# The final norm's two products: from GpSimd and ScalarE to one VectorE operation per tile, in a two-layer streaming encoder on Trainium2

## The reference, cut to what matters

```python
def rmsnorm(x, g):
    xf = x.astype(jnp.float32)
    y = xf * lax.rsqrt(jnp.mean(xf * xf, axis=-1, keepdims=True) + NORM_EPS)
    return (y * g.astype(jnp.float32)).astype(x.dtype)

for l in range(DEPTH):
    ...
    h_p = h_p + hier_moe(rmsnorm(h_p, norm_ffn[l]).reshape(b * t, d), *mw).reshape(b, t, d)
    h_s = h_s + hier_moe(rmsnorm(h_s, norm_ffn[l]).reshape(bd * td, d), *mw).reshape(bd, td, d)
y_prompt = rmsnorm(h_p, norm_final)
y_sample = rmsnorm(h_s, norm_final)
```

## Time and profile before

| what | us |
|---|---|
| median of three runs (lowest, highest) | 1415.55 (1410.67, 1418.3) |
| the profiled execution | 1415.48 |
| its span, first to last instruction | 1413.7 |
| PE busy in the span | 1225.1 (87%) |
| DVE busy | 468.2 (33%) |
| ACT busy | 285.8 (20%) |
| POOL busy | 165.9 (12%) |

### The profile page before, as it was taken

The page is one execution under the profiler, slowest core; times in us unless marked ns, Lnnn a source line. Parts: engine busy times, 40 slices in busy tenths (PEclk is TensorE's granted clock), DMA queues, the critical chain, the costliest instruction groups (busy, mean ns, idle before and its releaser), DMA issues.

```text
span 1413.7 us, 30382 instructions
## 1 busy us (share of the span) xinstructions
PE 1225.1 (87%) x13325; PEld 774.2 (55%) x13325; DVE 468.2 (33%) x1125; ACT 285.8 (20%) x714; POOL 165.9 (12%) x216
## 2 busy tenths in 40 slices
PE   6988899958999999948998799989886999999960
PEld 4444355547777777724444444444546777777740
DVE  4477652251000000025356651374633000000007
ACT  2123252110000000012345530242310000000013
POOL 1211120010000000020122221110001000000014
PEclk9889899969999999969999799999876999999995
DMA  9100040069999999953003101030028999999943
GB/s 302 14 10 2 1 182 30 16 230 357 371 401 397 393 389 406 349 195 112 16 15 122 69 16 45 30 124 16 30 78 286 353 401 403 396 392 396 381 157 145
DMA packets 73427, 283.73 MB, mean 201 GB/s; under 512 B 20205, under 2 KB 21277, under 8 KB 65098
## 3 DMA queue, kind: packets, MB, share of 16 engines
q1 hardware_dynamic: 56190, 237.94, 43.8%
q0 software_dynamic: 9216, 31.11, 6.4%
q10 hardware_dynamic: 7884, 12.65, 2.6%
HBM read 257.20 MB, written 24.48 MB: 199 GB/s over the span
## 4 chain that ended last, share of the span: by engine, by line
PE 67%; DVE 10%; DMA 9%; issue 9%; POOL 3%; ACT 1%; SPq 0%; ACTq 0%; POOLq 0%; DVEq 0%
PE bank L1135 22%; PE bank L850 13%; PE bank L1151 10%; PE bank L1061 8%; DMA slot<-in_moe_w 6%; PE bank L1007 2%; PE bank L974 2%; PE bank L1120 2%; PE bank L881 2%; POOL slot L2089 2%; PE bank L983 1%; DVE h L1948 1%; DVE slot L1649 1%; DVE stats L1648 1%; PE bank L873 1%
## 5 line engine op out<-in xcount | busy, mean ns | idle before, releaser
L1135 PE MATMUL bank<-arena,slot 128*64 128x96 f32 x8192 | 355.6, 249 | 13.9 <-issue 7.4
L1135 PEld LDWEIGHTS bank<-arena,slot 128*64 128x64 f32 x8192 | 346.8, 139 | 21.8 <-issue 12.3
L850 PE MATMUL bank<-slot,xT 128*128 128x512 f32 x512 | 240.6, 626 | 4.5 <-ACT slot L1325 3.3
L850 PEld LDWEIGHTS bank<-slot,xT 128*128 128x128 f32 x512 | 100.5, 202 | 125.0 <-issue 123.0
L1932 DVE TENSOR_TENSOR arena<-arena,bank 128x384 f32<-128x384 f32 x32 | 17.7, 554 | 406.6 <-ACT arena L1430 207.7
L1151 PE MATMUL bank<-slot,arena 128*32 128x512 f32 x1056 | 137.1, 594 | 0.4 <-issue 0.4
L1061 PE MATMUL bank<-slot,normed 128*128 128x512 f32 x256 | 116.6, 609 | 2.6 <-issue 1.3
L1430 ACT ACTIVATE arena<-bank 128x384 f32<-128x384 f32 x32 | 15.7, 490 | 396.3 <-PE bank L1135 396.3
L1061 PEld LDWEIGHTS bank<-slot,normed 128*128 128x128 f32 x256 | 48.6, 195 | 59.0 <-issue 58.3
L2135 POOL DMA_INDIRECT arena<-normed_rows,arena x32 | 29.1, 908 | 408.1 <-PE bank L1120 374.0
L1151 PEld LDWEIGHTS bank<-slot,arena 128*32 128x32 f32 x1056 | 38.5, 110 | 66.9 <-issue 64.0
(11 more groups left out here) (181 smaller groups left out, 1148.8 us busy)
## 6 DMA issues: line engine op xcount, KB each, us to landing
slot<-in_moe_w SPq DMA_DIRECT2D x86, 2048.0 KB, 17.8
xT<-in_moe_w SPq DMA_DIRECT2D x10, 2048.0 KB, 23.8
slot<-in_w_in_odd SPq DMA_DIRECT2D x6, 2048.0 KB, 13.6
slot<-in_w_in_even SPq DMA_DIRECT2D x3, 2048.0 KB, 13.6
expert_rows<-arena ACTq DMA_DIRECT2D x32, 192.0 KB, 10.2
slot<-in_w_out_even SPq DMA_DIRECT2D x2, 2048.0 KB, 11.6
normed_rows<-slot POOLq DMA_DIRECT2D x8, 512.0 KB, 2.9
expert_rows<-arena ACTq DMA_DIRECT2D x32, 128.0 KB, 8.5
```

The lines of the kernel that those rows point to most:

```text
L850: last = nc.tensor.matmul(b[o:o + wide, 0:n], xT[:, k, P * t + o:P * t + o + wide], w[:, k, 0:n], start=(k == 0), stop=(k == KC - 1))
L1135: last = nc.tensor.matmul(bank[o:o + 64, b, CAP * m:CAP * m + CAP], weights(w[par])[:, k, at_:at_ + 64], xgT[:, par, k, :], start=(k == 0) ...
```

## The change

Step Z moves from ACT to DVE, and POOL's `gain` is gone. DVE's new step Z is one scalar_tensor_tensor per tile, `h` times the row's inverse root times `gfin`, five in all. `gained` is gone; the wait for `gfin_in` now stands on DVE.

```diff
--- before.py
+++ after.py
@@ -538,7 +538,6 @@
         rows_known = sem("rows_known")
         lists_in = sem("lists_in")
         mask_ready = sem("mask_ready")
-        gained = sem("gained")
         scale_ready = sem("scale_ready")
         fin_ready = sem("fin_ready")
         act_step = sem("act_step")
@@ -1477,13 +1476,6 @@
                     taken(act, key)
                     act.dma_start(dst[0, 0], row[0:HIST, :]).then_inc(out_pool, 16)
 
-            def step_Z(t):
-
-                act.wait_ge(gained, t + 1)
-                act.wait_ge(scale_ready, t + 1)
-                y = fin[0:ROWS[t], t, :]
-                nc.scalar.activation(y, y, ACT.Copy, scale=rstd[0:ROWS[t], 4, t:t + 1]).then_inc(fin_ready, 1)
-
             def step_lambda():
                 act.wait_ge(lam_dots, 1)
                 nc.scalar.activation(lam_exp, lam_dot, ACT.Exp).then_inc(lam_exps, 1)
@@ -1516,8 +1508,6 @@
                 elif kind == "experts":
                     experts(*a)
                     log_and_exp_table()
-                elif kind == "Z":
-                    step_Z(*a)
                 elif kind == "lambda":
                     step_lambda()
 
@@ -1950,6 +1940,14 @@
                       .then_inc(h_added, 1)
                     dve.wait_ge(h_added, 2 * NT * l + 2 * t + c + 1)
 
+            def step_Z(t):
+                r = ROWS[t]
+                if t == 0:
+                    dve.wait_ge(gfin_in, 16)
+                nc.vector.scalar_tensor_tensor(out=fin[0:r, t, :], in0=h[0:r, t, :], scalar=rstd[0:r, 4, t:t + 1],
+                                               in1=gfin[0:r, :], op0=ALU.mult, op1=ALU.mult)\
+                  .then_inc(fin_ready, 1)
+
             def experts(l):
                 full = crowded(dve, l)
                 with dve.If(full):
@@ -1989,6 +1987,8 @@
                     step_y(*a)
                 elif kind == "C":
                     step_C(*a)
+                elif kind == "Z":
+                    step_Z(*a)
                 elif kind == "R":
                     if a == [0, 0]:
                         dve.wait_ge(small_in, 16 * SMALL_LOADS)
@@ -2119,14 +2119,6 @@
                         link(ins)
                     src, width = dst, 2 * width
 
-            def gain(t):
-
-                r = ROWS[t]
-                if t == 0:
-                    pool.wait_ge(gfin_in, 16)
-                pool.wait_ge(h_added, 2 * NT + 2 * (t + 1))
-                gtt(fin[0:r, t, :], h[0:r, t, :], gfin[0:r, :], ALU.mult).then_inc(gained, 1)
-
             def own_tokens(l):
                 all_x_stored(pool, l)
                 for e in range(NE):
@@ -2167,8 +2159,6 @@
                     step_X(*a)
                 elif kind == "Us":
                     sums(*a)
-                elif kind == "C" and a[0] == 1:
-                    gain(a[1])
                 elif kind == "experts":
                     experts(*a)
 
```

## The result

The changed kernel takes 1404.45 us (median of eight runs, 1401.89 to 1407.05); the kernel before took 1415.67 us in the same series (eight runs, 1408.38 to 1418.84). The medians lie 11.2 us apart. The ratio, taken from the means, is 0.9926 with a 95% interval of 0.9906 to 0.9946: 0.74% faster, about 10.4 us. The least gain that the interval allows is 0.54%, so the gain is clear of the prediction's bound of 0.5%, but by little. The prediction said 1406.7, a gain of 8.8 us.

The account below looks back on a forecast made before the run. The prediction took the final norm's DVE chain, held by POOL's products, and POOL's late DRAIN as the bound. Gains of 5.6 us on the chain and 3.2 at POOL's end took 1415.48 to 1406.7 us; range 1402.5 to 1412.

Parts of the forecast that it names:

- the prediction's bound of 0.5%: Whole kernel: about 0.5%, here 7.1 us, is what a measurement can tell from no change.
- The hold: Final norm's Newton steps: POOL's product holds DVE's two-input operation, 5.21 us in X0 and 2.21 in X1; goes with the products.
- Rival (c): Final norm: the long DVE operation is not POOL's doing and stays; DVE carries 1.32 more per tile, 1417.4 us; chance 0.06.
- Z at 1.28 to 1.32: DVE's five new steps in the final norm: 1.32 us each from start to start, 1.28 for the last.
- The gather holding X0 for 0.32 us: Final norm's first Newton step: POOL's last gather instruction holds DVE until 1384.39, so its operation ends at 1384.42, not 1384.10.
- Gathers and ACT hidden: Final norm: gathers land before DVE's C steps need them, C3's with 2.6 us to spare; ACT's root has 0.4 to spare.
- POOL's end off the path: Program's end: POOL's DRAIN over by 1392.5 or 1396.0, no longer behind SP's; 3.2 us gained.
- The estimate of 8.1 us: Program's end, kernel before: POOL's DRAIN goes on for 8.1 us after POOL's last product, over at about 1405.4.
- Rival (a): Program's end: POOL's DRAIN waits for something there, so 3.3 us behind SP's drain stay; 1409.9 us; chance 0.21.
- (b): Program's end: DVE's two-input operations slow POOL's DRAIN, whose 8.1 us count from 1402.5; 1412.6 us; chance 0.09.
- The sum: Whole change: 8.8 us off the span, 5.6 on the chain and 3.2 from POOL's end; time 1406.7 us.
- Work from DVE to ACT: Final norm: skill's rule for a saturated DVE, set aside because 1.99 of its 5.25 busy us per tile is holding.

Follow-up runs that it names:

- the early and the late small product: Changed kernel plus one 32x1 POOL product: early, behind Z1, one run, 1407.58 us; late, at the very end behind Z4, 1411.59 us.

## Why the prediction was right, point by point

- **The hold was POOL's, through DVE's second input, and went with the products.** Right: shown by putting them back (both holds return), by memsets (no hold) and by one-input operations (the hold moves). Rival (c), the hold staying, is out: L1545 is short in all 25 places.
- **Z at 1.28 to 1.32.** The length was right, 1.283. The distance was not: I took 1.32 from start to start from two operations with a semaphore between them. Behind Z, DVE does not wait for Z's own end, and the next operation starts 1.20 behind its start (1382.67 to 1383.87), below even the lower bound of 1.28. Four times 0.12 is 0.5 us.
- **The gather holding X0 for 0.32 us.** Wrong, and it was an inference from one row. The earlier trace rows show L1555 starting half a microsecond ahead of the product and not getting through, from which I took it that the gather held it. Without products it passes beside the gather in 0.22, in five profiles. In the kernel with the products kept, too, L1546 began 0.53 ahead of the first product's record and was held. So the hold seems to begin before the record of POOL's product: by at least 0.3 us, since an operation of 0.22 would have been through by then (1384.41 against 1384.72). How much more is not shown. With this term and the one above (0.32 + 0.48 = 0.80) the predicted 18.79 us from X0 to the end of Z4 becomes 17.99; measured 18.04. What is left is small slips: the sum for X0 leaves out the 0.03 us between the end of L1555 and L1557, X takes 0.83 per tile where 0.81 was counted, and C4 takes 2.61 where 2.64 was. The Trainium skill's inference (SBUF — State Buffer, "Who interferes with whom"), that descriptor generation does not take the read side, stands by these five profiles.
- **Gathers and ACT hidden.** Right: DVE has no gap from 1381.84 to 1399.88.
- **POOL's end off the path, worth 3.2 us.** Right: from the end of the last scaling to the end of the span it was 5.6 us before and is 2.3 now. The estimate of 8.1 us rested on POOL's last product before, which ends at 1405.43:

```profile
1403.09 2.34 POOL L2128 TENSOR_TENSOR normed<-h,slot 32x1024 f32<-32x1024 f32 x1 [3.10 <-DVE h L1948]
```

  The DRAIN itself was 7.992, four times, in kernels where it begins with nothing ahead of it, and its end lay 8.1 to 8.2 us behind that of POOL's last operation. Rival (a), that POOL's end keeps its distance, is out by the early and the late small product. So is (b): beside a DVE that never pauses, the DRAIN of the early product still took 7.992.
- **The sum.** Predicted tail 21.2, measured 20.4; predicted gain 8.8 us, 9.6 by the trace, 10.4 by the runs with an interval from 7.6 to 13.3. Both mis-sized terms erred the same way, so nothing cancelled. Of the 2.25 us by which the median came out below 1406.7, 0.8 are theirs; the rest lies within the scatter of the runs and speaks neither for nor against the prediction.
- **Work from DVE to ACT.** The prediction set this aside because 1.99 of DVE's 5.25 us was holding. That left out what comes after the change: without the holds DVE still runs 18 us without a gap, and the Newton step on ACT took 2.2 us off the tail.

## What to carry to other kernels

A cheap operation that is long in one place is not dear but blocked: look what another engine was doing until the same moment, and ask which of its neighbours pass. Work moved off DVE onto GpSimd can cost more than it saves while DVE's own operations need two inputs from SBUF; here 1.2 us per tile on DVE replaced a product of 2.3 that stopped it, and work that DVE does itself can be cheaper than work that it is kept waiting for. And the end of a program is a race between engines: the last store is not the end if another engine's own finish comes later, and in a program like this one GpSimd should have its last work more than 8 us before the last store has landed.

## What the runs showed of the hardware that I had not expected

- POOL's DRAIN at the program's end takes 7.992 us once its last compute operation is over, the same for 32 numbers, for a product of 32x1024 and for a memset, while the DRAIN at the start of the same programs takes 0.18. What it does in that time was not found: all these programs issue DMAs from POOL, and one without them was not tried. Where a gather was POOL's last work, the DRAIN's end lay 8.0 us behind the gather instruction's end in three kernels, and 8.5 in the profile of the changed kernel.
- The hold between DVE and POOL goes both ways: a product of POOL on 32 numbers took 0.77 us in place of 0.18, until the two-input operation of DVE that had started first was over.
- A 32x1024 operation on DVE takes 1.27 us against 1.28 for 128x1024, and POOL's product 2.34 for both: the small tile costs as much as a full one in this tail.
- Two large DVE operations without a wait between them start 1.20 us apart though each is recorded as 1.28 long.
